# Fewer page transfers, and the gated attention's rows of z loaded during the latent attention

## The chip, the cores and the metric

One core of a Trainium2 chip runs the whole kernel. The metric is the device time of one execution in microseconds, as the median of several runs; lower is better. Everything is float32.

## What is computed

One layer of a hybrid decoder for 512 prompt tokens and 64 sample tokens (8 sequences of 8). The reference, cut to what the change concerns:

```
z = rmsnorm(x) @ w_in                    # columns: latent attention | q, k, v, gate rows of the gated attention
mla_o = latent attention(z[:, :832])     # sample: over 16 pages of 128 cached tokens for each sequence
    s = (q_lat . lat_pool[page_table] + q_rope . kr_pool[page_table]) * ir_pool[page_table] * scale
gla_o = gated linear attention(z[:, 832:], state)
h = x + concat(rmsnorm(mla_o), gla_o) @ w_out
h = h + peer(rmsnorm(h))                 # per token and head: top 16 of 16384 experts; dots with rows of peer_u,
                                         # then the weighted sum of rows of peer_v
y = h + sigmoid(rmsnorm(h) @ w_ple_gate) * (p @ w_ple_proj)
```

The paged cache has, for each token, 256 latents, 64 rotated key values and 8 inverse key norms (inverse RMS).

## The kernel before

The 576 tokens are five tiles: 0 to 3 of the prompt, 4 (`PT`, 64 rows) of the sample. They pass the *front* (input projection, latent attention, gated attention, output projection, query projection, routing) in three groups: [0], [1, 2], [3, 4]. Group 1's input projection (`ahead`, L1208 on TensorE) is woven into group 0's front.

Behind the front runs the expert layer, the bulk of the bytes. For each unit (tile and head; tile 4 packs two heads) GpSimd issues 16 gathers of 128 rows of `peer_u` and 16 of `peer_v` (`gathers`, L2420), 1 MiB each, into a ring of eight buffers: 576 units' dots on VectorE (L1871) and 576 steps of the weighted sum (L1896), 1152 *rows* of work in all. A gather may start once VectorE has used the buffer eight before. A tile's gathers need its routes (`route_ready`), and its rows of `xrow` (L2380, one load for a tile of the prompt).

VectorE and ScalarE do both, the front's steps and the expert rows. VectorE's order is a table: `ROWS_BEFORE` says before which row each step of the front is done; `STEPS_BEFORE` does so for ScalarE, `CHAIN_BEFORE_PIECE` and `CHAIN_BEFORE_COPY` for the weaving in group 0, and `PAGES_BEFORE` says before which gather GpSimd issues each page transfer. Nothing is chosen at run time: an engine waits at the head of its own list.

**Pages (tile 4).** Each sequence's 16 pages come in two halves of eight (`pages_until`, L2402), each by three indirect transfers, of the latents (1 MB), the rope keys (256 KB) and the inverse RMS (32 KB), on GpSimd's queue among the gathers. Five half buffers are in turn. TensorE waits for all three of a half before `turn` (L1000, L1001, transposes), then come `score` (L1012 to L1014), the weighted sum (L1040) and its denominator (L1043). The indices `page_rows` are made by VectorE at the start from `page_table`. The mask `smask` is loaded with the constants (L539).

**Gated attention.** The SyncE queue (SP) waits until all outputs of the group's latent attention are stored and, in groups 0 and 1, its keys are parked in DRAM. Then it issues the gate weights, the state `S0` and the first tile's z (128 x 3088, 1.5 MB) to the one place `gz`. The next tile's z goes out after the first one's `gla_read` and the store of its output `go`; for tile 4 behind the output of the final prompt state too:

```
for t in tiles:
    if t != tiles[0]:
        e.wait_ge(s("gla_read"), t)
    e.dma_start(gz[:ROWS[t], :], z_dram[rows(t), MLA_COLS:IN_COLS]).then_inc(s("gla_z_loaded"), 16)
...
    e.wait_ge(s("gla_o_ready"), t + 1)
```

On VectorE the steps of a tile are: fills (L1464, L1465, first tile alone), gate (L1573, L1574, L1578), levels (L1604 to L1617, L1648, L1654), state update (L1664), output (L1691, L1694). TensorE begins a tile with transposes of z (L1086 to L1090), ScalarE ends it with L2195, which is followed by `gla_read`.

## Time and profile before

| | us |
|---|---|
| median of three runs | 4427.2 |
| lowest and highest | 4423.9, 4427.7 |
| the profiled execution, own time | 4432.5 |
| its span, first to last instruction | 4430.7 |

Mean granted clock of TensorE over the span: 0.719. 1599.5 MB move, 1268.3 of them on GpSimd's queue. The rows below give stretches of this span, in us from its start. A row of a chain or a timeline begins with the start and the duration. In a window's row a busy time in us is followed by the number of instructions begun in it.

### The profile page before, as it was taken

The page shows a single profiled execution, that of the slowest core. Times are in us where ns is not written, and L with a number is a line of the kernel's source. Part 1 is how long each engine was busy: PE and PEld are TensorE (multiplying, and loading weights), DVE is VectorE, ACT ScalarE, POOL GpSimd, SP SyncE. Part 2 cuts the span into 40 slices and gives each one's busy share as a digit, 9 for nine tenths or more (in the row PEclk, how much of TensorE's full clock was granted, in tenths as well). Part 3 has the DMA queues.
Part 4 walks back from the last instruction along what each step waited for, and adds up shares of the span by engine and source line. Part 5 has one row for each costly group of instructions (what it writes and reads, how often), then busy time and mean ns, then how long its engine had stood idle before and what let it go on. Part 6 is the DMA issues. An engine that isn't in the chain of part 4 may idle for free.

```text
span 4430.7 us, 24002 instructions
## 1 busy us (share of the span) xinstructions
PE 2274.9 (51%) x8206; PEld 1357.4 (31%) x8206; DVE 3288.9 (74%) x3698; ACT 516.6 (12%) x1093; POOL 2182.4 (49%) x1232
## 2 busy tenths in 40 slices
PE   8999715424989482678882339720000570000916
PEld 4457403222475131366662213620000230000402
DVE  0130699898566988866889875699999879988682
ACT  2120102122012001211111110100000100001000
POOL 0000365644231546566775563435668547877370
PEclk9999856556999796767665559865555785555957
DMA  8667889988996999979898999998899999999995
GB/s 285 245 234 273 322 351 351 381 360 322 420 388 269 410 414 411 360 284 361 317 379 355 370 367 421 419 366 332 353 399 405 404 422 423 422 403 421 422 418 184
DMA packets 261537, 1599.50 MB, mean 361 GB/s; under 512 B 28019, under 2 KB 49715, under 8 KB 92134
## 3 DMA queue, kind: packets, MB, share of 16 engines
q0 software_dynamic: 176448, 1268.30, 70.8%
q1 hardware_dynamic: 83078, 320.63, 19.2%
q10 hardware_dynamic: 1888, 9.03, 0.5%
q8 instruction: 65, 1.06, 0.1%
q14 instruction: 58, 0.48, 0.0%
HBM read 1554.75 MB, written 42.56 MB: 361 GB/s over the span
## 4 chain that ended last, share of the span: by engine, by line
PE 33%; DVE 27%; DMA 15%; POOL 14%; issue 7%; ACT 2%; SPq 1%; another core or an unknown queue 0%; DVEq 0%; ACTq 0%; POOLq 0%
PE bank L796 15%; POOL ring L2420 13%; DVE total L1896 9%; DVE ring L1871 8%; DMA ring<-in_peer_v,idx_all 5%; PE bank L1208 4%; PE bank L1171 4%; DMA ring<-in_peer_u,idx_all 4%; DMA front<-z_dram 1%; PE bank L770 1%; PE bank L850 1%; POOL front L2402 1%; PE bank L1040 1%; DMA front<-in_cache_k_inv_rms,page_rows 1%; PE bank L1014 1%
## 5 line engine op out<-in xcount | busy, mean ns | idle before, releaser
L1896 DVE SCALAR_TENSOR_TENSOR total<-ring,gate_all,total 128x2048 f32<-128x2048 f32 x571 | 1342.0, 2350 | 190.9 <-DMA ring<-in_peer_v,idx_all 166.4
L2420 POOL DMA_INDIRECT ring<-in_peer_u,idx_all x576 | 1062.8, 1845 | 822.6 <-DVE dots L1871 352.8
L1871 DVE CUSTOM_DVE_ANT_0 ring<-ring,xrow 128x2048 f32<-128x2048 f32 x576 | 1298.2, 2286 | 205.3 <-DMA ring<-in_peer_u,idx_all 202.5
L2420 POOL DMA_INDIRECT ring<-in_peer_v,idx_all x576 | 1003.0, 1741 | 746.4 <-DVE total L1896 327.6
L796 PE MATMUL bank<-front 128*128 128x512 f32 (+3 forms) x2048 | 896.1, 595 | 77.2 <-ACT front L2009 71.8
L770 PE MATMUL bank<-inv_diag,front 128*128 128x128 f32 (+1 forms) x336 | 66.3, 382 | 1286.7 <-DVE inv_diag L1294 1218.7
L796 PEld LDWEIGHTS bank<-front 128*128 128x128 f32 (+1 forms) x2048 | 356.6, 178 | 605.7 <-issue 600.6
L770 PEld LDWEIGHTS bank<-inv_diag,front 128*128 128x128 f32 (+1 forms) x336 | 63.0, 290 | 1292.3 <-DVE inv_diag L1294 1214.2
L1171 PE MATMUL bank<-front 128*128 128x128 f32 (+2 forms) x1536 | 256.7, 329 | 19.1 <-DMA front<-in_peer_w_q 17.4
L1171 PEld LDWEIGHTS bank<-front 128*128 128x128 f32 x1536 | 239.5, 192 | 37.8 <-DMA front<-in_peer_w_q 20.3
L2443 POOL DMA_DIRECT2D ring<-in_w_in x12 | 10.8, 902 | 366.4 <-PE bank L1208 239.2
L1292 DVE RECIPROCAL st<-st 128x1 f32<-128x1 f32 (+1 forms) x20 | 3.2, 161 | 219.2 <-ACT st L1961 219.2
L1208 PE MATMUL bank<-ring 128*128 128x490 f32 x384 | 163.8, 574 | 2.1 <-ACT front L2009 2.1
L2364 ACT ACTIVATE dots<-dots 128x16 f32<-128x16 f32 x36 | 7.7, 215 | 997.9 <-DVE dots L1871 954.1
L834 PE MATMUL bank<-ident,front 128*128 128x128 f32 (+1 forms) x20 | 4.6, 380 | 184.8 <-DVE front L1342 93.1
L1000 PE MATMUL bank<-ident,front 128*128 128x128 f32 x256 | 75.5, 397 | 40.6 <-DMA front<-in_cache_k_inv_rms,page_rows 34.8
L1208 PEld LDWEIGHTS bank<-ring 128*128 128x128 f32 x384 | 70.4, 190 | 74.9 <-issue 71.8
L2380 POOL DMA_DIRECT2D xrow<-xn_dram x6 | 3.4, 576 | 179.1 <-DMA z_dram<-total 102.5
L1116 PE MATMUL bank<-front 128*128 128x128 f32 (+1 forms) x288 | 42.7, 321 | 90.8 <-DVE front L1605 79.6
L1487 DVE MAX8 front<-front 128x8 f32<-128x128 f32 (+1 forms) x80 | 19.2, 280 | 91.7 <-ACT front L2219 91.1
L1331 DVE TENSOR_TENSOR g_mla<-g_mla 128x128 f32<-128x128 f32 x1 | 0.3, 291 | 100.5 <-DMA g_mla<-in_qk_gain_q 100.5
L1040 PE MATMUL bank<-front 128*64 128x256 f32 x256 | 69.7, 440 | 7.9 <-ACT front L2251 7.9
(306 smaller groups left out, 2889.4 us busy)
## 6 DMA issues: line engine op xcount, KB each, us to landing
front<-in_w_in SPq DMA_DIRECT2D x64, 980.0 KB, 6.9
front<-in_w_out SPq DMA_DIRECT2D x48, 1024.0 KB, 9.1
front<-in_peer_w_q SPq DMA_DIRECT2D x48, 1024.0 KB, 13.5
front<-in_w_ple_gate SPq DMA_DIRECT2D x48, 1024.0 KB, 9.0
ring<-in_w_in POOLq DMA_DIRECT2D x12, 1960.0 KB, 10.1
front<-in_w_uq SPq DMA_DIRECT2D x6, 1536.0 KB
ring<-in_peer_u,idx_all POOLq DMA_INDIRECT x576
ring<-in_peer_v,idx_all POOLq DMA_INDIRECT x576
```

Source lines behind the costliest of these rows:

```text
L770: mm = e.matmul(out, row, inv_diag[:R, :R], start=True, stop=True)
L796: mm = e.matmul(bank[4 * sl + c][:R, 0:ncol], XT[:, k, sl * P:sl * P + R], W[:, n % SLABS, c * ncol:(c + 1) * ncol], start=(k == 0), stop= ...
L850: mm = e.matmul(bank[j][:R, 0:2 * QK], cqT[:, slot(t), k, 0:R], wq[:, k, j * 2 * QK:(j + 1) * 2 * QK], start=(k == 0), stop=(k == 3))
L1000: e.transpose(bank[k][:, j * P:(j + 1) * P], latb[:, i, k * P:(k + 1) * P], ident[:, :])
L1014: mm = e.matmul(S, lt[0:ROPE, 2, j * P:(j + 1) * P], qrT[0:ROPE, b, :], start=False, stop=True)
L1040: e.matmul(bank[7][0:NS, 0:KVR], pTs[:, pg, :], latb[:, pg % HALF, :], start=(pg == 0), stop=False)
L1171: mm = e.matmul(bank[j][:, 0:ntok], W[:, n % SLABS, at:at + P], XT[:, k, 0:ntok], start=(k == 0), stop=(k == KD - 1))
L1208: mm = e.matmul(bank[6 + sl][:, 0:IN_BANK], xt[:, k, sl * P:(sl + 1) * P], chunk(n)[:, k % 8, :], start=(k == 0), stop=(k == KD - 1))
L1871: e.tensor_tensor_reduce(out=ring[:, b, :], in0=ring[:, b, :], in1=xrow[:, t % 2, :], scale=1.0, scalar=0.0, op0=ALU.mult, op1=ALU.add, ac ...
L1896: e.scalar_tensor_tensor(out=total, in0=ring[:, b, :], scalar=c1, in1=total, op0=ALU.mult, op1=ALU.add).then_inc(s("summed"), 1)
L2402: e.indirect_dma_start(out=dst.rearrange("p i d -> p (i d)"), out_offset=None, in_=a[pool][0].rearrange("n (r i) d -> (n r) (i d)", r=16), ...
L2420: e.indirect_dma_start(out=ring[:, k % RING, :], out_offset=None, in_=a[("peer_u", "peer_v")[side]][0], in_offset=bass.IndirectOffsetOnAxi ...
```

## The change

1. **Page transfers.** The inverse RMS of all pages goes to a buffer of its own, by eight transfers (one for each sequence, 64 KB) at the program's start on GpSimd's queue. The rope keys come by one transfer of 512 KB for each sequence, with its first half, into one of three buffers. The latents stay as they were, 16 of 1 MB. Index rows are made for sequences (8) and halves (16).
2. **Mask.** `smask` is loaded before `w_uk` of the sample attention, no longer with the constants.
3. **z of the gated attention.** In groups 0 and 1 SP issues the gate weights, `S0` and the first tile's z before it waits for the last output of the latent attention, when the last values are projected (`v_ready`); in group 2 where it did before. The second tile's z goes out once the first one's has landed, to another place: tiles 0, 1 and 4 use `gz_first`, 2 and 3 `gz_other`. The places of the other gated buffers are shuffled for that. TensorE gets a wait for the state of the tile before; VectorE waits for the stores and the parked keys itself before its fills.
4. **Tables.** All five are planned anew.

```
 PAGE_BUFS = 5
+KR_BUFS = 3
...
-PAGES_BEFORE = [390, 396, 396, 399, 399, 415, 419, 431, 431, 442, 447, 453, 463, 469, 469, 480]
+PAGES_BEFORE = [395, 395, 395, 402, 404, 414, 414, 426, 428, 440, 440, 451, 452, 462, 467, 476]
...
-        page_ids = sb("page_ids", [P, 2 * DEC_B * HALF], I32)
-        page_rows = sb("page_rows", [P, 2 * DEC_B], U32)
+        page_ids = ring[:, 4, 0:DEC_B * N_PAGES].bitcast(I32)
+
+        page_rows = sb("page_rows", [P, 3 * DEC_B], U32)
+        page_irms = sb("page_irms", [P, DEC_B, N_PAGES * H_MLA])
...
-            pages_sb.append((carve(HALF, KVR), carve(HALF, ROPE), carve(HALF, H_MLA)))
+            pages_sb.append(carve(HALF, KVR))
+        smask = carve(DEC_B, NS)
+        kr_sb = [carve(N_PAGES, ROPE) for _ in range(KR_BUFS)]
...
-        gz = carve(GLA_COLS, at=0)
+
+        gz_first = carve(GLA_COLS, at=half0)
...
+        gz_other = carve(GLA_COLS, at=0)
+
+        def gz_at(t):
+
+            return gz_other if t == PT - 1 or slot(t) and t != PT else gz_first
...
+        def pages_landed(u):
+
+            return 16 * sum(2 - v % 2 for v in range(u % PAGE_BUFS, u + 1, PAGE_BUFS))
...
-            e.dma_start(smask[:, :, :].rearrange("p a b -> p (a b)"), c["smask"]).then_inc(s("consts_loaded"), 16)
...
+                def gated_loads():
+                    e.dma_start(w_ga[0:GATE_R, :], a["w_gla_a"][0]).then_inc(s("gla_w_loaded"), 16)
+                    e.dma_start(w_ga[GATE_R:GATE_R + 1, :], a["b_gla_a"][0].rearrange("(o n) -> o n", o=1)).then_inc(s("gla_w_loaded"), 16)
+                    if g:
+                        e.dma_start(S0, s_dram).then_inc(s("gla_w_loaded"), 16)
+                    t = tiles[0]
+                    e.dma_start(gz_at(t)[:ROWS[t], :], z_dram[rows(t), MLA_COLS:IN_COLS]).then_inc(s("gla_z_loaded"), 16)
+
...
+                        if hh and t == tiles[-1] and PT not in tiles:
+                            e.wait_ge(s("v_ready"), PHALVES[hh, t] + 1)
+                            gated_loads()
...
                     e.wait_ge(s("sample_qT_psum"), 2)
+                    e.dma_start(smask.rearrange("p a b -> p (a b)"), c["smask"]).then_inc(s("sample_w_loaded"), 16)
                     e.dma_start(wuk_f, a["w_uk"][0].rearrange("(k p) h d -> p k (h d)", p=P)).then_inc(s("sample_w_loaded"), 16)
...
-                e.dma_start(w_ga[0:GATE_R, :], a["w_gla_a"][0]).then_inc(s("gla_w_loaded"), 16)
-                e.dma_start(w_ga[GATE_R:GATE_R + 1, :], a["b_gla_a"][0].rearrange("(o n) -> o n", o=1)).then_inc(s("gla_w_loaded"), 16)
-                if g:
-                    e.dma_start(S0, s_dram).then_inc(s("gla_w_loaded"), 16)
+                if PT in tiles:
+                    gated_loads()
...
-                    if t != tiles[0]:
+                    if t == tiles[0] and len(tiles) > 1:
+                        e.wait_ge(s("gla_z_loaded"), 16 * (t + 1))
+                        e.dma_start(gz_at(t + 1)[:ROWS[t + 1], :], z_dram[rows(t + 1), MLA_COLS:IN_COLS]).then_inc(s("gla_z_loaded"), 16)
+                    if t == PT:
                         e.wait_ge(s("gla_read"), t)
-                    e.dma_start(gz[:ROWS[t], :], z_dram[rows(t), MLA_COLS:IN_COLS]).then_inc(s("gla_z_loaded"), 16)
-                    if t == PT:
...
-                    latb, krb, _ = pages_sb[u % PAGE_BUFS]
+                    latb, krb = pages_sb[u % PAGE_BUFS], kr_sb[u // 2 % KR_BUFS]
                     if n % 2 == 0:
-                        e.wait_ge(s(f"pages_landed{u % PAGE_BUFS}"), 16 * 3 * (u // PAGE_BUFS + 1))
+                        e.wait_ge(s(f"pages_landed{u % PAGE_BUFS}"), pages_landed(u))
...
                     if t:
                         e.wait_ge(s("gla_read"), t)
+                        e.wait_ge(s("gla_state"), H_GLA * t)
...
                 e.wait_ge(s("o_stored"), O_STORED[g])
+                e.wait_ge(s("mla_outputs"), 16 * 2 * (tiles[-1] + 1))
+                e.wait_ge(s("lat_stored"), 16 * (tiles[-1] + 1))
+                if g < LAST:
+                    e.wait_ge(s("keys_parked"), 16 * 6 * (g + 1))
                 e.wait_ge(s("gla_w_loaded"), 32 * (g + 1) + 16 * g)
...
-                    ir = pages_sb[(2 * b + half) % PAGE_BUFS][2].rearrange("p g h -> p (g h)")
+                    if b == 0 and half == 0:
+                        e.wait_ge(s("page_irms_loaded"), 16 * DEC_B)
+                    ir = page_irms[:, b, half * HALF * H_MLA:(half + 1) * HALF * H_MLA]
...
-            link(e.tensor_scalar(page_at, page_at, 16.0, in_page[:, :], ALU.mult, ALU.add))
+            link(e.tensor_copy(page_f, page_ids.rearrange("p (u q) -> p u q", q=N_PAGES)))
+            link(e.tensor_tensor(page_f, page_f, which_page.unsqueeze(1).to_broadcast([P, DEC_B, N_PAGES]), ALU.mult))
+            link(e.tensor_reduce(page_at[:, 0:DEC_B], page_f, AX, ALU.add))
+            link(e.tensor_scalar(page_at[:, 0:DEC_B], page_at[:, 0:DEC_B], float(HALF), in_page[:, :], ALU.mult, ALU.add))
+            halves_at = page_at[:, DEC_B:3 * DEC_B].rearrange("p (u h) -> p u h", h=2)
+            mark(e.tensor_scalar(halves_at[:, :, 0], page_at[:, 0:DEC_B], 2.0, None, ALU.mult))
+            link(e.tensor_scalar(halves_at[:, :, 1], page_at[:, 0:DEC_B], 2.0, 1.0, ALU.mult, ALU.add))
...
+            def pages(dst, pool, tokens, at):
+
+                return e.indirect_dma_start(out=dst, out_offset=None,
+                                            in_=a[pool][0].rearrange("n (r i) d -> (n r) (i d)", i=tokens),
+                                            in_offset=bass.IndirectOffsetOnAxis(ap=page_rows[:, at:at + 1], axis=0))
...
-                    for dst, pool in zip(pages_sb[u % PAGE_BUFS], ("cache_kv_latent", "cache_k_rope", "cache_k_inv_rms")):
-                        e.indirect_dma_start(out=dst.rearrange("p i d -> p (i d)"), out_offset=None,
-                                             in_=a[pool][0].rearrange("n (r i) d -> (n r) (i d)", r=16),
-                                             in_offset=bass.IndirectOffsetOnAxis(ap=page_rows[:, u:u + 1], axis=0))\
+                    b = u // 2
+                    if u % 2 == 0:
+                        if b >= KR_BUFS:
+                            e.wait_ge(s("latT_psum"), 4 * (b - KR_BUFS) + 4)
+                        pages(kr_sb[b % KR_BUFS].rearrange("p i d -> p (i d)"), "cache_k_rope", 2 * HALF, b)\
                             .then_inc(s(f"pages_landed{u % PAGE_BUFS}"), 16)
+                    pages(pages_sb[u % PAGE_BUFS].rearrange("p i d -> p (i d)"), "cache_kv_latent", HALF, DEC_B + u)\
+                        .then_inc(s(f"pages_landed{u % PAGE_BUFS}"), 16)
 
...
             e.wait_ge(s("page_rows_ready"), 1)
+            for b in range(DEC_B):
+                pages(page_irms[:, b, :], "cache_k_inv_rms", 2 * HALF, b).then_inc(s("page_irms_loaded"), 16)
```

How instructions move, at three places. SP in group 1, from the last output stores of the latent attention to the output projection's input; before:

```order
L598 DMA mix_dram<-front 128x512 x2
L606 DMA kt_dram<-front 512x1x256
L607 DMA ktr_dram<-front 256x1x256
L608 DMA v_dram<-front 128x1024
L612 DMA out_ir_p<-ms 128x8 x2
L633 DMA front<-in_w_gla_a 16x512
L634 DMA front<-in_b_gla_a 1x512
L636 DMA front<-s_dram 128x1024
L644 DMA front<-z_dram 128x3088
L655 DMA mix_dram<-front 128x1024
L644 DMA front<-z_dram 128x3088
L655 DMA mix_dram<-front 128x1024
```

and in the change:

```order
L625 DMA mix_dram<-front 128x512
L608 DMA front<-in_w_gla_a 16x512
L609 DMA front<-in_b_gla_a 1x512
L611 DMA front<-s_dram 128x1024
L613 DMA front<-z_dram 128x3088
L625 DMA mix_dram<-front 128x512
L633 DMA kt_dram<-front 512x1x256
L634 DMA ktr_dram<-front 256x1x256
L635 DMA v_dram<-front 128x1024
L639 DMA out_ir_p<-ms 128x8 x2
L670 DMA front<-z_dram 128x3088
L682 DMA mix_dram<-front 128x1024 x2
```

The first z went ahead of the last output of the latent attention, the second ahead of the first gated output.

VectorE in group 1, from the output of the first tile (L1694, now L1728) to the gate of the second (L1573, now L1607); a dot product with a row of peer_u is two rows of this list. Before, where nine dot products stand between the two:

```order
L1691 RECIPROCAL ms<-ms 128x4
L1694 SCALAR_TENSOR_TENSOR front<-bank,ms,front 128x256 x4
L1871 ISA ring,dots<-ring,xrow 128x2048
L1871 ISA dots 128x1
...
L1573 TENSOR_SCALAR front<-bank 128x512
L1574 SCALAR_TENSOR_TENSOR front<-front 128x512
```

and in the change:

```order
L1725 RECIPROCAL ms<-ms 128x4
L1728 SCALAR_TENSOR_TENSOR front<-bank,ms,front 128x256 x4
L1933 SCALAR_TENSOR_TENSOR total<-ring,gate_all,total 128x2048
L1908 ISA ring,dots<-ring,xrow 128x2048
L1908 ISA dots 128x1
L1607 TENSOR_SCALAR front<-bank 128x512
L1608 SCALAR_TENSOR_TENSOR front<-front 128x512
```

Nine rows became two. Counted in rows of expert work done before a step: the fills of group 1 124, now 125; the gate of its second tile 153, now 145; its mix norms 173, now 165. In group 2 the output of tile 3 stands at 528, now 533, the gate of tile 4 at 536, now 543; the last routing step of tile 4 at 848, now 831, the first norm of the embedding at 858, now 840.

GpSimd, where the page transfers begin among the gathers of one unit; before:

```order
L2420 DMA ring<-in_peer_v,idx_all 128x2048 x6
L2402 DMA front<-in_cache_kv_latent,page_rows 128x2048
L2402 DMA front<-in_cache_k_rope,page_rows 128x512
L2402 DMA front<-in_cache_k_inv_rms,page_rows 128x64
L2420 DMA ring<-in_peer_v,idx_all 128x2048 x6
L2402 DMA front<-in_cache_kv_latent,page_rows 128x2048
```

and in the change:

```order
L2465 DMA ring<-in_peer_v,idx_all 128x2048 x11
L2422 DMA front<-in_cache_k_rope,page_rows 128x1024
L2422 DMA front<-in_cache_kv_latent,page_rows 128x2048 x2
L2422 DMA front<-in_cache_k_rope,page_rows 128x1024
L2422 DMA front<-in_cache_kv_latent,page_rows 128x2048
L2465 DMA ring<-in_peer_v,idx_all 128x2048 x5
```

Of three transfers a half, two or one are left, and they begin five gathers later.

## Rows read from the trace of the kernel before

**Rows 1.** The page: busy shares of the engines, and the span in 40 slices.
```profile
PE 2274.9 (51%) x8206; PEld 1357.4 (31%) x8206; DVE 3288.9 (74%) x3698; ACT 516.6 (12%) x1093; POOL 2182.4 (49%) x1232
...
GB/s 285 245 234 273 322 351 351 381 360 322 420 388 269 410 414 411 360 284 361 317 379 355 370 367 421 419 366 332 353 399 405 404 422 423 422 403 421 422 418 184
```

**Rows 2.** Windows: seven stretches, busy us of each engine (instructions), clock, DMA.
```profile
590.00:1385.00 795.00, 439.86 (x1594) 296.46 (x1594) 622.14 (x655) 153.88 (x319) 357.46 (x210) 0.72 0.89 358
...
1883.00:2337.00 454.00, 360.45 (x1873) 292.54 (x1873) 336.18 (x280) 73.35 (x138) 326.70 (x172) 0.67 0.85 336
...
2900.00:3410.00 510.00, 9.84 (x79) 9.18 (x77) 496.16 (x711) 12.10 (x27) 311.29 (x178) 0.51 0.92 367
3410.00:4330.00 920.00, 273.25 (x712) 132.39 (x712) 766.91 (x528) 45.99 (x112) 592.66 (x315) 0.65 1.01 417
```

**Rows 3.** Waits of POOL: us in total, times, longest us.
```profile
POOL ring L2443 <- PE bank L796: 127.3, 1, 127.3
POOL xrow L2380 <- DMA z_dram<-total: 102.5, 1, 102.5
POOL xrow L2380 <- DVEq L1789: 76.5, 1, 76.5
```

**Rows 4.** Chain that ended last, between the tiles of group 1: start us, us, what.
```profile
962.91 0.31 ACT ms L2195
...
965.51 12.85 DMA front<-z_dram
...
978.40 0.38 PE bank L1086
```

**Rows 5.** The page, costliest groups: the two kinds of row work.
```profile
L1896 DVE SCALAR_TENSOR_TENSOR total<-ring,gate_all,total 128x2048 f32<-128x2048 f32 x571 | 1342.0, 2350 | 190.9 <-DMA ring<-in_peer_v,idx_all 166.4
...
L1871 DVE CUSTOM_DVE_ANT_0 ring<-ring,xrow 128x2048 f32<-128x2048 f32 x576 | 1298.2, 2286 | 205.3 <-DMA ring<-in_peer_u,idx_all 202.5
```

**Rows 6.** Windows: two stretches of group 1's projections.
```profile
1100.00:1150.00 50.00, 50.00 (x118) 22.16 (x117) 27.74 (x24) 0.00 (x0) 11.25 (x12) 1.00 1.01 421
...
1300.00:1385.00 85.00, 74.80 (x368) 64.83 (x366) 41.68 (x90) 22.25 (x57) 2.54 (x4) 0.90 0.61 233
```

**Rows 7.** Timeline of DVE, fills and last state update of group 1's first gated attention.
```profile
887.57 0.17 DVE L1464 MEMSET front<- 17x128 f32 x1
...
959.84 0.86 DVE L1664 SCALAR_TENSOR_TENSOR front<-front,bank 128x256 f32<-128x256 f32 x2
```

**Rows 8.** Waits of PE, 2337 to 2560 us.
```profile
PE bank L1086 <- DMA front<-z_dram: 27.0, 1, 27.0
```

**Rows 9.** Groups by line, 1883 to 2337 us: POOL's transfers of rope keys and inverse RMS.
```profile
L2402 POOL DMA_INDIRECT front<-in_cache_k_rope,page_rows x16 | 38.8, 2422 | 4.9 <-issue 4.9
L2402 POOL DMA_INDIRECT front<-in_cache_k_inv_rms,page_rows x16 | 34.9, 2180 | 4.9 <-issue 4.9
```

**Rows 10.** Waits of PE and then of POOL, 1883 to 2337 us.
```profile
PE bank L1000 <- DMA front<-in_cache_k_inv_rms,page_rows: 34.8, 6, 12.1
...
POOL ring L2420 <- DVE total L1896: 57.9, 10, 21.8
```

**Rows 11.** The same chain, 1880 to 2460 us: the four landings of page transfers.
```profile
2003.31 10.95 DMA front<-in_cache_k_inv_rms,page_rows
...
2063.80 3.50 DMA front<-in_cache_k_inv_rms,page_rows
...
2148.10 9.70 DMA front<-in_cache_k_inv_rms,page_rows
...
2207.11 8.30 DMA front<-in_cache_k_inv_rms,page_rows
```

**Rows 12.** Timeline of POOL, issues of three page transfers.
```profile
2000.81 0.94 POOL L2402 DMA_INDIRECT front<-in_cache_kv_latent,page_rows  x1 [0.30 <-issue]
...
2003.31 9.13 POOL L2402 DMA_INDIRECT front<-in_cache_k_inv_rms,page_rows  x1 [0.30 <-issue]
...
2066.19 2.08 POOL L2402 DMA_INDIRECT front<-in_cache_kv_latent,page_rows  x1 [0.30 <-issue]
```

52 lines of the change are left out of this document (25 added, 27 removed), and 64 rows, old and new, of tables (CHAIN_BEFORE_PIECE, ROWS_BEFORE).

## The prediction

> **What bounds the kernel now.** I began with the page's busy shares and forty slices [rows 1]. No engine is full over the span: VectorE (DVE) has 74%, TensorE (PE) 51%, GpSimd (POOL) 49%. But the DMA engines move 422 GB/s in the best slices and hold that in the last quarter. The windows by stretch say why [rows 2]. From 3410 us on the gathers run at 417 GB/s: DMA bounds. From 2900 to 3410 us DVE is busy 496.2 of 510 us: routing the last tiles beside the row work bounds. In the latent attention of the sample tile (1883 to 2337 us) neither is full: DVE 336.2 of 454 us, DMA 336 GB/s. In 590 to 1385 us, group 1's front, DMA moves 358 GB/s. Idle DMA time at 422 GB/s: 454 x (1 - 336/422) = 92.5 us in the first of these, 795 x (1 - 358/422) = 120.6 us in the second. Time can be won only where both DVE and DMA stand partly idle.
>
> One thing more bounds group 1's front. POOL stood 76.5 us before one load of xrow [rows 3]: it had fetched all that tile 0 and its routes allowed, and waited for the first route of tile 1. So what shortens the chain from group 1's latent attention to its route comes off the total one to one, until that wait is gone. Before the first gather PE is the bound, with work waiting.
>
> **The change part by part.**
>
> *z of the second tile of group 1: -15.0 us.* Before, SP issues that load only after the output store of the first tile. ACT's root that raises gla_read ended at 963.2 (962.91 + 0.31), z landed at 978.36, PE began at 978.40 [rows 4]. In the change the load goes out while tile 1 runs, to a place of its own, and PE starts at about 963.4: 978.4 - 963.4 = 15.0 us. PE's new wait for gla_state is over by then: DVE's last L1664 ended at 960.7 [rows 7]. Queued behind it on PE is only this tile's own work. Nothing is lost on DVE: between the two tiles it took nine rows, now two; the seven, at 2.29 to 2.35 us each [rows 5], are done later, in the stretch where PE projects (1056 to 1385 us). There DVE is idle anyway and DMA, over 1300 to 1385 us, moves 233 GB/s [rows 6], 38 us of idle transfer time; seven rows ask 7 x 2.49 = 17.4 us of it (1 MiB at 422 GB/s).
>
> *First tile's z, gate weights and state, fetched earlier: 0.* PE could start sooner, but DVE does its fills at 887.57 [rows 7], when the table lets it, and the table still does so at the same row (124 before, 125 now). DVE's added waits for the small outputs and parked keys cost nothing: SP waited for the same ones before it issued the loads for which DVE then waited.
>
> *z of tile 4 (group 2): 0, bounds -27.0 and 0.* PE waited 27.0 us for it [rows 8], behind the state's output. The load now goes out during tile 3. But no route is waited for later: POOL's xrow waits are two, this tile's is not among them [rows 3]. The new table also puts ten rows, not eight, between the two tiles' steps on DVE. A shorter chain with slack behind it gives nothing, so I take the upper end.
>
> *Pages: -12.5 us, bounds 0 and -34.8.* Before, 48 page transfers stand in POOL's queue among the gathers of that stretch. The change leaves 24: the 16 of inverse RMS become 8 at the program's start, the 16 of rope keys become 8. By their means that takes 34.9 + 38.8/2 = 54.3 us off POOL, and 24 gaps of 0.30 make 61.5 [rows 9, 12]. PE waited 34.8 us in six waits for pages [rows 10]. Four landings stand on the chain that ended last, 10.95, 3.50, 9.70 and 8.30 us [rows 11], each behind the third transfer of its half. Per half 1.5 transfers fewer at 2.08 + 0.30 us (what most cost beside DVE's row work [rows 12]) is 3.57 us; four make 14.3. Back go two larger key transfers (256 KB more, 0.6 us each at 422 GB/s) and 0.6 for the mask, now loaded just ahead of w_uk, for which PE waits: -14.3 + 1.2 + 0.6 = -12.5. The lower end is all that PE waited; the upper that the ring of eight row buffers takes the place of the page: POOL waited 57.9 us for DVE's sums there too [rows 10]. I stand nearer the middle, since only four waits were on the chain.
> The Trainium skill, DMA: Bandwidth & Descriptors, section on the anatomy of a DMA from the GpSimd queue, gives a fixed part of about 2.0 us and bytes over 436 GB/s. By this a 32 KB transfer lands 2.1 us after it starts, and four of them off the chain would be 8.4 us, a total of some 4406. The trace's four landings are longer (3.50 to 10.95 us), so the row decides.
>
> *The eight early transfers: 0.* POOL's first wait is 127.3 us long, for PE [rows 3]; they fit ahead of it. They move 0.5 MB, 1.2 us of DMA, beside a stretch where PE is the chain. *Mask out of the constants: 0.* One load of 256 KB less ahead of x, 0.6 us of DMA at 422 GB/s.
>
> *Replanned tables: 0, upper end +45.* The routing of tile 4 and the first embedding's norms are packed: by row 840, not 858. Those 18 rows lie in or just after the stretch where DVE is full [rows 2]. DVE's work is the same, only sooner, and DMA still has idle time to give.
>
> **Sum**, against the profiled execution's own time: 4432.5 - 15.0 - 12.5 = 4405.0. The median of the three runs is 5.3 us below that execution, so I forecast 4400 (4399.7).
>
> **Rivals.**
> *More: POOL was the limit of the latent stretch.* For it: the same kind of issue takes 0.94, 2.08 or 9.13 us [rows 12], the long one while DVE ran row after row without a gap, and DMA stands idle meanwhile. Removing an issue removes such a stall. Then all 34.8 us of page waits go, 22 more than forecast: 4378; with some of tile 4's z, 4370. Against: POOL also waited 57.9 us for DVE there.
> The Trainium skill, SBUF: State Buffer, section Who interferes with whom, says that a DVE instruction with two SBUF inputs blocks a GpSimd instruction only if that one reads SBUF, and then fully. An indirect transfer reads its indices there. The 9.13 us issue agrees with a full block, and by this rule this rival is what should happen.
> *Less: the pages give nothing.* The next gather's buffer, still held by DVE, is what POOL then waits for. 4427.2 - 15.0 = 4412.
> *None: the weights pay.* In 1100 to 1150 us DMA is at 421 GB/s, gathers and w_out together [rows 6]. Seven more gathers there are 17.4 us of transfer; if they delay the weights, not the idle end, PE's projection gets longer by as much, and group 1's 15 us are gone. With the pages giving nothing too: 4427. Against: PE's projection shows no such wait, it is busy 50 of 50 us there [rows 6]. It is also the case in which the change does not do what it says: a z load held in SP's queue behind the keys' stores and landing late, which at 15 us to spare would also end here.
> *Slower: the packed routing.* In 2900 to 3410 us DVE is at 97%, DMA at 367 GB/s. If routing steps are set closer than the ring of eight rows can bridge, DMA stops, and no later stretch gives that back, for there DMA is full. At worst each of 18 rows costs its 2.49 us: 4400 + 45 = 4445. It decides from 12 rows on (30 us against the 27.5 won). Against: ring and DVE rate stay, and the table was already dense.
>
> **How the numbers follow.** Forecast (4388 to 4411): 0.40. More (4365 to 4388): 0.19. Less (4412): 0.14. None (4427): 0.15. Slower (around 4445): 0.12. 0.2% is 8.9 us, about what a measurement of this kernel can tell from no change. The first three are faster: 0.73; same 0.15; slower 0.12. The range leaves out the far end of "more" and nearly all of "slower": 4368 to 4430.
>
> **What would show it.** In the profile after: PE's wait for z between the tiles of group 1 gone, the next gate matmul about 15 us after the last output matmul less than before; POOL's wait for the second xrow earlier by 15 us and about 60 long; 24 page issues, not 48, in the latent stretch, a page wait of PE of some 20 us or less, that stretch shorter than 454 us; DVE's full stretch not longer than before by more than 10 us. I am wrong if POOL's route wait ends where it did, if PE waits in L796 for weights, or if the latent stretch keeps its length with POOL waiting longer for DVE.

## The result and the profile after

The changed kernel takes 4347.0 us (median of four runs, 4345.2 to 4349.3) against 4426.4 us for the kernel before (four runs, 4423.9 to 4427.7): the ratio is 0.9822, interval 0.9805 to 0.9839, some 79 us faster. I forecast 4400 and a range down to 4368: the sign is right, the size is not, and the time lies below that range. The profiled execution has a span of 4346.4 us (before 4430.7) and a mean granted clock of 0.727 (before 0.719).

The page of the changed kernel, busy shares and forty slices (compare [rows 1]):

```profile
PE 2255.6 (52%) x8206; PEld 1342.1 (31%) x8206; DVE 3289.2 (76%) x3700; ACT 521.2 (12%) x1097; POOL 2204.8 (51%) x1216
...
GB/s 295 251 221 286 307 357 362 415 326 338 424 424 294 423 424 411 348 353 362 407 377 357 347 402 413 409 346 343 399 362 404 424 423 422 422 402 423 423 415 181
```

DVE has the same work (3289 us), PE about 19 us less of busy time for the same 8206 matmuls. The slices that were at 284 and 317 GB/s in the latent stretch are gone.

Windows of the changed kernel, the stretches of [rows 2] between the same steps of VectorE; the columns are the same:

```profile
578.00:1350.00 772.00, 437.83 (x1589) 295.17 (x1590) 628.42 (x648) 148.90 (x310) 372.60 (x213) 0.73 0.92 373
1847.00:2253.00 406.00, 333.82 (x1865) 271.49 (x1865) 328.01 (x275) 70.92 (x135) 307.56 (x149) 0.73 0.93 374
2820.00:3330.00 510.00, 14.32 (x105) 13.42 (x103) 501.32 (x725) 14.87 (x30) 296.88 (x174) 0.52 0.92 370
3330.00:4250.00 920.00, 276.13 (x712) 133.85 (x712) 764.86 (x516) 51.02 (x116) 600.89 (x318) 0.65 1.01 416
```

Group 1's front is 23 us shorter, the latent stretch 48 us. The two last stretches are as before. Not all of that reaches the end: the rows of work are the same 1152, and what one stretch does sooner the next may not need sooner. So I also counted the rows of work (in the changed kernel L1908, L1933 and, for the first step of a sum, L1931) in each trace, from 0, and compared when row n ended. This table gives the end time in the kernel before, and the difference to it, in us:

| row of work | before | changed |
|---|---|---|
| 96 | 815.3 | -20.8 |
| 192 | 1148.5 | -4.9 |
| 256 | 1468.0 | -38.0 |
| 384 | 1894.0 | -36.9 |
| 480 | 2265.3 | -80.5 |
| 640 | 2823.0 | -77.6 |
| 832 | 3402.0 | -67.2 |
| 928 | 3702.9 | -83.6 |
| 1151 | 4339.3 | -84.4 |

In these two traces about 37 us come from group 1's front and 41 to 44 us from the latent stretch; my terms were 15.0 and 12.5. Some 22 us of the second gain are there only against this trace of the kernel before, not against its second one (below).

The signs I had named. Waits of POOL in the changed kernel (compare [rows 3]), and one line of its timeline:

```profile
POOL xrow L2417 <- DMA z_dram<-total: 102.5, 1, 102.5
...
POOL xrow L2417 <- DVEq L1823: 60.4, 1, 60.4
```

```profile
1350.97 0.56 POOL L2417 DMA_DIRECT2D xrow<-xn_dram  x1 [60.38 <-DVEq L1823]
```

The wait for tile 1's route is 60.4 us long, as forecast (some 60), but that is luck: it ends 33 us earlier than the 1384.0 of before, not 15, and it also begins 17 us earlier. Its length does not come from the early z. With both edits under the old tables it is as long as before, and with all z late under the new tables as short as here (the kernels "changed, tables as before" and "changed, all z late" below):

```profile
POOL xrow L2417 <- DVEq L1823: 77.8, 1, 77.8
```

```profile
POOL xrow L2416 <- DVEq L1822: 62.1, 1, 62.1
```

In every kernel with the new rows of group 1 it is 57 to 62 us long, in every one with the old rows 77 to 78.

The page transfers and PE's wait for them, 1847 to 2253 us (compare [rows 9, 10]):

```profile
L2422 POOL DMA_INDIRECT front<-in_cache_kv_latent,page_rows x16 | 27.8, 1740 | 11.8 <-PE bank L1071 8.1 <-issue 3.7
L2422 POOL DMA_INDIRECT front<-in_cache_k_rope,page_rows x8 | 15.2, 1902 | 2.4 <-issue 2.4
```

```profile
PE bank L999 <- DMA front<-in_w_uk: 16.0, 1, 16.0
...
PE bank L1027 <- DMA front<-in_cache_kv_latent,page_rows: 9.1, 3, 5.9
```

24 issues, and 9.1 us of page waits instead of 34.8.

### The profile page after: what moved, and what is told of

Same layout as the page of the kernel before. It is cut to its first block, busy times and chain, and to the rows that moved or that the text cites. A ratio compares the mean times of both kernels' runs of the same rounds, so it can differ in the third digit from the quotient of the medians.

```text
span 4346.4 us, 23992 instructions
## 1 busy us (share of the span) xinstructions
PE 2255.6 (52%) x8206; PEld 1342.1 (31%) x8206; DVE 3289.2 (76%) x3700; ACT 521.2 (12%) x1097; POOL 2204.8 (51%) x1216
## 4 chain that ended last, share of the span: by engine, by line
PE 34%; DVE 30%; POOL 16%; DMA 10%; issue 7%; ACT 2%; SPq 0%; DVEq 0%; ACTq 0%; POOLq 0%
PE bank L823 18%; POOL ring L2465 15%; DVE ring L1908 11%; DVE total L1933 9%; PE bank L1199 4%; DMA ring<-in_peer_u,idx_all 3%; PE bank L1236 3%; DMA ring<-in_peer_v,idx_all 3%; PE bank L797 1%; PE bank L877 1%; DMA front<-in_cache_kv_latent,page_rows 1%; PE bank L1027 1%; PE bank L947 1%; PE bank L1041 1%; DVE front L1531 1%
## 5 line engine op out<-in xcount | busy, mean ns | idle before, releaser
L1933 DVE SCALAR_TENSOR_TENSOR total<-ring,gate_all,total 128x2048 f32<-128x2048 f32 x571 | 1342.0, 2350 | 179.5 <-DMA ring<-in_peer_v,idx_all 154.6
L2465 POOL DMA_INDIRECT ring<-in_peer_v,idx_all x576 | 1074.1, 1865 | 699.0 <-DVE total L1933 358.2
L1908 DVE CUSTOM_DVE_ANT_0 ring<-ring,xrow 128x2048 f32<-128x2048 f32 x576 | 1297.5, 2287 | 172.9 <-DMA ring<-in_peer_u,idx_all 171.0
```

Source lines behind the costliest of these rows:

```text
L1908: e.tensor_tensor_reduce(out=ring[:, b, :], in0=ring[:, b, :], in1=xrow[:, t % 2, :], scale=1.0, scalar=0.0, op0=ALU.mult, op1=ALU.add, ac ...
L1933: e.scalar_tensor_tensor(out=total, in0=ring[:, b, :], scalar=c1, in1=total, op0=ALU.mult, op1=ALU.add).then_inc(s("summed"), 1)
L2465: e.indirect_dma_start(out=ring[:, k % RING, :], out_offset=None, in_=a[("peer_u", "peer_v")[side]][0], in_offset=bass.IndirectOffsetOnAxi ...
```

## Experiments

Two theories stood at the start. **Edits:** early z and fewer page transfers win the time, the tables only follow. **Pair:** VectorE works through a fixed list, so an edit that makes an input early pays only as far as the table also puts the step that uses it at an earlier row; and an earlier row pays only if the input is there. All eighteen runs, with the kernel before run beside them on the same chip (rows with the same time of the kernel before make one block, run on one chip; the changed kernel itself was run in the first comparison and in "changed, again"):

| kernel | median us | kernel before | ratio, interval |
|---|---|---|---|
| changed, tables as before | 4385.7 | 4415.1 | 0.9925 to 0.9965 |
| before, new tables | 4391.1 | 4415.1 | 0.9941 to 0.9967 |
| changed, 48 page transfers | 4363.0 | 4415.1 | 0.9873 to 0.9909 |
| changed, all z late | 4367.4 | 4415.1 | 0.9882 to 0.9916 |
| **changed, again** | 4345.1 | 4411.0 | 0.9826 to 0.9864 |
| before, again (one run) | 4406.9 | 4411.0 | |
| new tables for group 1 alone | 4364.0 | 4411.0 | 0.9859 to 0.9903 |
| tail of the table as before | 4345.2 | 4411.0 | 0.9814 to 0.9864 |
| first z late | 4351.1 | 4407.4 | 0.9848 to 0.9894 |
| z of tile 2 late | 4366.8 | 4407.4 | 0.9878 to 0.9926 |
| old start of group 1 | 4359.8 | 4407.4 | 0.9860 to 0.9904 |
| gaps between dot products | 4347.1 | 4407.4 | 0.9841 to 0.9883 |
| z of tile 4 late | 4353.1 | 4424.8 | 0.9829 to 0.9859 |
| new start, old rows of group 1 | 4373.5 | 4424.8 | 0.9871 to 0.9901 |
| page table as before | 4400.1 | 4424.8 | 0.9925 to 0.9955 |
| early z alone, tables as before | 4401.7 | 4424.8 | 0.9948 to 0.9975 |
| new page table, old rows | 4352.6 | 4412.6 | 0.9834 to 0.9874 |
| pages two gathers sooner | 4351.4 | 4412.6 | 0.9840 to 0.9877 |

### The two kernels again

> The changed kernel once more, unedited, so that the parts are compared on one chip: 0.982 of the kernel before, as in the first comparison.

> The kernel before once more, unedited, for its trace on this chip. By every theory the times of its rows of work lie within some 10 us of the first trace's; where they do not, that much of the differences so far is the chip and not the edit.

The changed kernel repeats within 2 us, and its rows of work end within 3 us of the first trace's. The kernel before does not, and I had expected its traces within some 10 us: its second trace (span 4405.1) is within 3 us of the first up to row 384, 23.6 us ahead at row 480 and 25.0 at the end. Its medians on the chips used lie between 4407.4 and 4426.4. So some 22 of the 84 us between the first two traces are how the old kernel's latent stretch happened to go in that one. Where I compare traces below, it is with the second one of before: there the changed kernel (second trace) is 35.3 us ahead at row 384, 52.6 at row 640 and 62.1 at the end.

### Edits alone, tables alone

The edit of the first: the five lists of the kernel before in the changed kernel; of the second: the new lists in the kernel before.

```
 # changed kernel
-ROWS_BEFORE, STEPS_BEFORE, PAGES_BEFORE, CHAIN_BEFORE_PIECE, CHAIN_BEFORE_COPY = new
+ROWS_BEFORE, STEPS_BEFORE, PAGES_BEFORE, CHAIN_BEFORE_PIECE, CHAIN_BEFORE_COPY = as before
```

> The changed kernel with all five tables of the kernel before. Theory A (the edits themselves win the time, the tables only follow): 4345 to 4360 us, nearly all of the 79 us. Theory B (the edits make room, and only the new tables use it: they start group 1's front earlier and set the latent stretch closer): 4395 to 4412 us, that is 15 to 30 us won. Theory C (the tables alone): 4427 us.

> The kernel before with all five tables of the changed one: the replanning alone. Theory A: 4420 to 4440 us, no gain. Theory B: part of the gain, 4385 to 4410 us (group 1's earlier start of some 24 us survives, but VectorE then waits in its closer list for z and for pages). Theory C: 4347 us, all of it.

4385.7 and 4391.1 us: 29.4 and 24.0 us below the kernel before by medians (by the ratios 24 and 20). Together they give 66 us on the second chip (4411.0 to 4345.1) and 79 on the first. What the pair theory expected came true for the second kernel; the first came out 9 us below its lower end, on a chip where the kernel before is 11 us faster too. That edits alone, or tables alone, carry the gain falls: each has under half of it. But the two halves nearly make the whole. By the last row of the traces the edits alone are 28.0 us ahead of the second trace of before, the tables alone 22.9, both together 62.1. So 11 us of the 62 are there only when both are (13 of 66 by medians). The pair theory holds for that part; the larger part each half wins by itself.

### Early z, taken apart

All late: the loads moved back to their places in the kernel before. First late: `gated_loads()` moved back. Tile 2 or tile 4 late: the second tile's load again behind the first one's output.

```
-                    if t == tiles[0] and len(tiles) > 1:
+                    if t == tiles[0] and len(tiles) > 1 and not (t + 1 == 2):
                         ... load of z of t + 1
+                    if t != tiles[0] and t == 2:
+                        e.wait_ge(s("gla_read"), t)
+                        ... load of z of t
```

> The changed kernel with z, gate weights and state loaded where they were before, in all groups (the first tile's behind the last output of the latent attention, the second's behind the first one's output), pages and tables as changed. By my forecast 15 us for tile 2 and nothing else: 4362 us. If the closer tables of group 1 need the early z, more: group 1's gated chain was 33 us earlier in the changed kernel, so up to 4380 us. If tile 4's z counts too (27 us of wait before), up to 4400 us.

> The changed kernel with only the first tile's gate weights, state and z in groups 0 and 1 back behind the last output of the latent attention; the second tile's follows it and still goes out early. By my prediction this part is worth 0: 4346 us. Rival: the new table puts VectorE's gated steps at earlier rows, so that a late first z makes VectorE itself stand still at the gate of tile 1; then part of the 21 us that all late loads cost (4367 us against 4346): 4352 to 4360 us.

> The changed kernel with only tile 2's z (second of group 1) behind the first tile's read and the store of its output, as before; tile 4's stays early. By my prediction this is worth 15 us: 4361 us. By the traces so far, with all z late VectorE stood 19.3 us at the gate of tile 2, a step that the new table puts 8 rows earlier: 4361 to 4366 us, and rows 160 to 256 some 18 us later.

> The changed kernel with only tile 4's z back behind the output of tile 3 and the final prompt state. By my prediction (no route is waited for later, a shorter chain with slack gives nothing) 0: 4346 us. Rival, the end that I left out of the sum: TensorE's 27.0 us of wait come off tile 4's chain, which the new table sets closer, so up to 4372 us with the late load.

All late costs some 21 us (4367.4 against 4345.1 to 4347.0), the first z alone 4 to 6, tile 2's z alone 20 to 22. (The changed kernel was not run in these blocks, so this rests on its two medians elsewhere.) Of tile 2's, 12.0 us are there at row 384 and 20.8 at row 640; what adds the rest on the way was not looked for. Tile 4's costs 6 to 8 by medians, but nothing by the ratio (0.9844 against 0.9845 for the changed kernel on its own chip), and its trace ends 5.6 us behind: between 0 and 8, not settled. PE waited 38.5 us for that z in its trace, and little of it came through.

What a late z does under the new table is in the waits of DVE of the kernel with all z late, 860 to 1000 us (columns: us in total, times, longest):

```profile
DVE front L1606 <- ACT front L2203: 19.1, 1, 19.1
```

L1606 is the gate of tile 2. The new table sends VectorE there at row 145, before at 153; z is not in, and VectorE itself stands 19.1 us with all its rows behind that step. What an early z does under the old table is in the waits of PE of the changed kernel with old tables, same stretch:

```profile
PE bank L1123 <- ACT front L2194: 45.3, 2, 44.7
PE bank L1128 <- DVE front L1608: 32.0, 2, 21.2
```

The wait for z has become one of 21.2 us for the same gate step, which VectorE's list reaches only at row 153. The timeline of DVE gives the start of that step in three kernels (the changed one, all z late, old tables):

```profile
954.04 0.69 DVE L1607 TENSOR_SCALAR front<-bank 128x512 f32<-128x512 f32 x1 [0.27 <-ACT front L2204]
```

```profile
971.97 0.69 DVE L1606 TENSOR_SCALAR front<-bank 128x512 f32<-128x512 f32 x1 [19.07 <-ACT front L2203]
```

```profile
979.73 0.69 DVE L1607 TENSOR_SCALAR front<-bank 128x512 f32<-128x512 f32 x1
```

From the fills of the group (874.3, 875.7, 883.1 us) that is 79.8, 96.3 and 96.6 us; in the kernel before 99.5 (887.6 to 987.0, [rows 7] has the fill). Counted from the fills, each half of the change wins 3 us at this step, both together 20. Counted from the start of the span the step begins at 987.0 us before (984.2 in the second trace), 979.7 with the old tables, 972.0 with all z late and 954.0 in the changed kernel, since the fills move too. With the old tables POOL's route wait ends at 1373.8 us (before 1384.0 and 1381.7), 8 to 10 us earlier.

### The table of group 1, taken apart

```
+ROWS_BEFORE = before[:96] + new[96:]                 # old start
+ROWS_BEFORE = new[:96] + before[96:347] + new[347:]  # new start, old rows
```

In the first of the two, ScalarE's first six numbers are as before too. In the second, three entries at the seam are one or two higher, so that the list does not fall.

> The changed kernel with the table of before for VectorE's first 96 steps (as far as row 95 of work: group 0's last routes and the start of group 1's latent attention) and ScalarE's first six numbers; all later steps as in the new table. The new table lets group 1's front start at row 18, the old one at row 25. If that earlier start carries group 1's gain beyond the early z (the changed kernel was 17.5 us ahead at row 96): 4358 to 4364 us. If the later rows of the table carry it (tile 2's gate at row 145, not 153): 4346 to 4350 us.

> The mirror of the old-start kernel: VectorE's first 96 steps as in the new table, its steps 96 to 346 (rows 95 to 345, the gated attention, output and query projection of group 1) as before, all later steps, ScalarE's and the pages' tables as new. If the two parts of the table add up (the early start some 12 us by row 384, the closer rows the other 12): 4357 to 4362 us. If the start alone carries it: 4347 us. If it is lost without the closer rows: 4366 us or more.

Without the earlier start (row 25 instead of 18) 4359.8 us, 13 to 15 worse. Without the closer rows 4373.5 us, 27 to 28 worse than the changed kernel's medians in other blocks, 20 worse than the kernel with tile 4's z late in its own; there PE waits again for VectorE at the gate, 860 to 1000 us:

```profile
PE bank L1096 <- DVE front L1576: 32.2, 2, 21.4
```

The traces at row 384, in us ahead of the second trace of before, separate the three things that make up group 1's gain:

| early z | closer rows | early start | ahead at row 384 |
|---|---|---|---|
| yes | no | no | 11.5 |
| yes | no | yes | 11.9 |
| yes | yes | no | 23.6 |
| yes | yes | yes | 35.3 |
| no | yes | yes | 17.0 |

The start is worth nothing (0.4 us) while VectorE's later rows are the old ones, and 11.7 us with the closer ones. The closer rows are worth 12.1 us with the old start and 23.4 with the new. Early z is worth 18.3 us under the new table. If the two parts of the table added up, the kernel without the closer rows would have been at 4357 to 4362 us. They don't: an explanation that fits is that a chain that starts sooner ends sooner only if none of its steps is held at an old row. One pair of traces does not fit so well: the kernel before with the new tables, which has no early z either, is only 10.5 us ahead at row 384, not 17.0. Where these 6.5 us come from was not tested.

### Pages and the tables of the latent stretch

48 transfers: keys and inverse RMS in halves again, three transfers for each half page set.

```
-                    if u % 2 == 0: pages(kr_sb[...], "cache_k_rope", 2 * HALF, b)
-                    pages(pages_sb[...], "cache_kv_latent", HALF, DEC_B + u)
+                    for dst, pool in (latents, half of the keys, half of the inverse RMS):
+                        pages(dst, pool, HALF, DEC_B + u)
```

> The changed kernel with 48 page transfers in the latent stretch again (rope keys and inverse RMS in halves, each half by three transfers), all else as changed. If pages were worth my 12.5 us: 4359 us. If GpSimd was the limit of that stretch, as my rival had it (34.8 us and more; the trace shows the stretch about 35 us shorter, with denser tables): 4380 to 4395 us. If pages gave nothing: 4347 us.

4363.0 us: the pages are worth 16 to 18 us by medians and 13 by the traces at the last row. My 12.5 was sized about right for the new tables.

The early z alone, with 48 transfers and the old tables:

> The changed kernel with the five tables of before and 48 page transfers in the latent stretch: early z alone, the first two terms of my prediction without any replanning. My forecast is -15.0 us for it; the trace with old tables and both edits was 11.5 us ahead at row 384: 11 to 15 us faster than the kernel before on the same chip, that is 4395 to 4402 us against 4411, and the rest up to the 4385.7 of both edits (10 to 16 us) is what the page edit gives under the old tables, where I forecast 12.5.

4401.7 us, 23.1 below the kernel before by medians, 17 by the ratio (0.9961), where I had expected 11 to 15; its trace is 11.1 us ahead at row 384 and 12.4 at the end. Against the kernel with both edits under the old tables (24 by its ratio, 29.4 by medians) the page edit has 6 or 7 us, by the traces' last rows 15.5. These numbers are too near the spread to be split further; the two edits together under the old tables are 24 to 29 us, and my sum was 27.5.

The tables there: those of before behind group 1 (VectorE's steps from 347 on, ScalarE's from unit 27 on, pages), then the same but with the new page table, then the old page table alone, then new pages two gathers sooner:

```
+ROWS_BEFORE = new[:347] + before[347:]; STEPS_BEFORE = new[:27] + before[27:]
+PAGES_BEFORE = before          # first and third kernel, new in the second
+PAGES_BEFORE = [n - 2 for n in new]   # fourth; rows new in the third and fourth
```

> The changed kernel with the new tables only as far as group 1's routing (347 of VectorE's 705 steps), the tables of before behind it. If each stretch's gain is its own: group 1's part stays (38 us by row 256, 37 at row 384 in the changed kernel) and the latent stretch keeps only what the page edit gives under the old table; with my 12.5 us for that, 4427 - 37 - 12.5 = 4377 us. If the latent stretch needs no new table: 4347 us.

> The changed kernel with the row and step tables of before behind group 1, as in the kernel of 4364.0 us, but with the new page table. If the page table carries the latent stretch's 19 us by itself: 4346 us. If it is the pair that counts (pages that keep ahead of VectorE's rows): the new page table is in the mean earlier than the old one, so TensorE's page waits (18.1 us there) fall, and the time stays between: 4352 to 4364 us. With the pair as cause and the old rows as the limit it does not get worse than 4364 us.

> The changed kernel with only the table of page transfers as before (before which gather each of the 16 goes out); the row and step tables stay new. The old tables behind group 1 cost 18.9 us (4364.0 against 4345.1). If the page table is what carries that: 4360 to 4365 us. If VectorE's rows carry it: 4345 to 4350 us.

> The changed kernel with each page transfer two gathers sooner. The old page table, up to 11 gathers later, cost 54 us. If pages still bind the stretch, this wins a little: 4338 to 4344 us. If TensorE's remaining 8.1 us of page waits are covered, or the queue then waits for a page buffer instead of gathering: 4346 to 4356 us.

4364.0, 4352.6, 4400.1 and 4351.4 us. The old rows and the old page table behind group 1 together cost 17 to 19 us (I had expected 0 or 30); the new page table gives 11 of them back, 8 by the traces. The old page table under the new rows costs 53 to 55 against the changed kernel's medians elsewhere, 47 against the kernel with tile 4's z late in its own block: thirteen of the sixteen halves come up to 11 gathers later (three come 3 to 5 sooner) while most of VectorE's steps sit 2 to 7 rows earlier. I had expected 15 to 20 at most. So the old page table is worse under new rows than under old ones (4400.1 against 4364.0): this is the clearest sign of a pair. The chip is one on which the kernel before, too, is slow (4424.8), and part of the cost may come from that. Waits of PE in that kernel, and its window from the start of the stretch to the fills of the gated attention:

```profile
PE bank L1027 <- DMA front<-in_cache_kv_latent,page_rows: 51.1, 6, 13.5
```

```profile
1844.00:2303.00 459.00, 355.66 (x1865) 289.22 (x1865) 328.02 (x273) 71.14 (x135) 287.61 (x149) 0.67 0.83 329
```

The same window in the changed kernel and in the second trace of the kernel before:

```profile
1847.00:2252.00 405.00, 333.82 (x1865) 271.49 (x1865) 327.29 (x272) 70.92 (x135) 307.09 (x149) 0.73 0.93 373
```

```profile
1885.00:2318.00 433.00, 354.84 (x1865) 288.17 (x1865) 336.98 (x280) 73.57 (x138) 328.28 (x170) 0.69 0.90 354
```

The first number after the stretch is its length, the next PE's busy time. All have 1865 matmuls, but PE is busy 334, 355 or 356 us for them. The granted clock goes with it: 0.73, 0.69, 0.67. In all rows of the next table busy time times clock lies between 237 and 245 us (worked out from them), so the busy time differs by the clock and not by the work. PE is busy for most of this stretch; that its slower matmuls lengthen it as its waits do is my reading, and no run tested it. Over the kernels:

| kernel | stretch, us | PE's page waits | PE busy | clock |
|---|---|---|---|---|
| before, first trace | 457 | 34.8 | 359.4 | 0.66 |
| before, second trace | 433 | 25.1 | 354.8 | 0.69 |
| page table as before | 459 | 51.1 | 355.7 | 0.67 |
| edits, old tables | 423 | 27.2 | 343.8 | 0.71 |
| before, new tables | 414 | 14.6 | 341.6 | 0.71 |
| changed, 48 transfers | 415 | 16.9 | 339.6 | 0.71 |
| changed | 405 | 9.1 | 333.8 | 0.73 |
| pages two gathers sooner | 401 | 6.6 | 332.4 | 0.73 |
| early z alone, tables as before | 439 | 27.0 | 348.2 | 0.69 |
| gaps between dot products | 401 | 2.1 | 339.1 | 0.72 |
| new tables for group 1 alone | 437 | 18.1 | 364.8 | 0.67 |
| new page table, old rows | 429 | 3.0 | 352.2 | 0.69 |

From the first to the changed kernel the stretch loses 52 us: 25.7 of page waits and 25.6 of PE's busy time. From the second trace of before it loses 28: 16.0 of page waits and 21.0 of busy time, and PE's other idle time grows by 9. So the even split of the first pair is no rule. In the rows above the last two, fewer page waits mostly go with a higher clock; the kernel with gaps, with the fewest of those waits and 0.72, does not quite fit. The last two show that pages are not the only thing that it goes with: there VectorE's steps come at the old rows, and PE's clock is 0.67 to 0.69 even with 3.0 us of page waits. What goes with the clock is a correlation here; no run held all else fixed. Two gathers sooner gains nothing more (4351.4; the stretch is 4 us shorter and the end is not earlier).

### The packed routing

```
+ROWS_BEFORE = new[:552] + before[552:]
```

> The changed kernel with the table of before from VectorE's step 552 on (rows 584 and later: the last routing and the first embedding's norms no longer packed). My rival (packed steps stop the gathers, 2.49 us for each of 18 rows) would make this faster than the changed kernel, by up to 45 us: 4302 us. If the packing costs nothing in the end (row 832 was 18 us late in the changed kernel's trace and row 928 on time again): 4347 us. If the packing was a gain: above 4352 us.

4345.2 against 4345.1 us: no difference. The traces show what happens in between. At row 832 the changed kernel is 43.8 us ahead of the second trace of before and this one 56.5, at row 928 60.2 and 58.4. The packed steps delay the rows by some 18 us between rows 800 and 832, and 16 of them come back by row 928, when the old table does its steps. Windows of this kernel, the stretch in which VectorE is full:

```profile
2820.00:3330.00 510.00, 8.60 (x71) 7.94 (x70) 496.21 (x709) 14.67 (x29) 311.09 (x179) 0.51 0.92 366
```

VectorE is busy 496 of 510 us there, 501 in the changed kernel: it is full with either order.

### Are GpSimd's long issues a bound?

In the latent stretch single issues of GpSimd last up to 11.6 us. POOL and DVE of the changed kernel (second trace), timeline from 2165 us:

```profile
2167.68 11.60 POOL L2465 DMA_INDIRECT ring<-in_peer_v,idx_all  x1 [3.00 <-DVE dots L1908]
2179.58 3.11 POOL L2465 DMA_INDIRECT ring<-in_peer_v,idx_all  x1 [0.30 <-issue]
```

```profile
2167.33 2.28 DVE L1908 CUSTOM_DVE_ANT_0 ring<-ring,xrow 128x2048 f32<-128x2048 f32 x1
...
2176.18 2.28 DVE L1908 CUSTOM_DVE_ANT_0 ring<-ring,xrow 128x2048 f32<-128x2048 f32 x1
...
2178.39 1.28 DVE L1572 TENSOR_TENSOR front<-front,bank 128x1088 f32<-128x1088 f32 x1
```

Five dot products run end to start (2167.33 to 2178.4), and the issue ends only when VectorE has gone on to an instruction with one input in PSUM. The experiment gives VectorE a gap after each dot product of rows 384 to 544:

```
                     e.tensor_tensor_reduce(... dots ...)
+                    if 384 <= rows_taken[0] < 544:
+                        link(e.memset(breath[:, :], 0.0))     # 1 x 1, and a wait for its end
                     row_taken()
```

> The changed kernel with a one-element fill of VectorE, and a wait for its end, behind each dot product of rows 384 to 544 (some 80). In the traces GpSimd's longest issues (4.4 to 14 us, 9 of them in this stretch) all last while VectorE runs dot products with no gap between them, and end with the burst. If the gap is what lets GpSimd in, no issue in these rows is longer than some 3 us. If those stalls bound the stretch, the time falls by 5 us or more, 4336 to 4341 us, although VectorE has some 10 us more to do; if the ring of eight rows covers them: 4346 to 4356 us.

The same place in this kernel, POOL:

```profile
2167.46 2.89 POOL L2468 DMA_INDIRECT ring<-in_peer_v,idx_all  x1 [4.98 <-DVE dots L1909]
2170.66 2.05 POOL L2468 DMA_INDIRECT ring<-in_peer_v,idx_all  x1 [0.30 <-issue]
2173.02 2.05 POOL L2468 DMA_INDIRECT ring<-in_peer_v,idx_all  x1 [0.30 <-issue]
```

One fill of 0.06 us with a wait for its end lets GpSimd in. Of nine issues over 4 us between 1600 and 2400 us (66 us) two are left (14 us), one of them ahead of row 384, where nothing was added; POOL's busy time in the stretch falls from 307 to 271 us. The time stays: 4347.1 us. In the changed kernel the stalls are real and do not bound the time; that it is the ring of eight rows that covers them is inferred. In the kernel before, with twice the page transfers, the gaps were not tried.

## Why the prediction was right or wrong

**z of the second tile of group 1, -15.0:** right in part. The load goes out early and PE's wait for z is gone, but it does not come off POOL's route wait one to one: that wait is as long as before (77.8 us) and begins and ends 8 to 12 us sooner when the tables are the old ones. The gate step stands at row 153 of VectorE's list there, and PE waited 21.2 us for it. All early z together was worth 11 to 13 us at row 384 under the old rows; with the closer rows tile 2's z alone is worth 20 to 22 us. My 15.0 lies between and fits neither.

**First tile's z, 0:** 4 to 6 us. I said the table does the fills at the same row. It does (124 and 125), but the rows themselves now come 13 us earlier, and then a late z costs a little. A row number is not a time.

**z of tile 4, 0, bounds -27 and 0:** 0 to 8 us, within the bounds.

**Pages, -12.5:** 13 to 18 us under the new tables, 6 to 15.5 under the old ones, so the size was about right; the way I built it left something out. I added up transfers on four landings of the chain. With all changes together the stretch got shorter by PE's page waits and also by PE's busy time at a higher clock: 25.7 and 25.6 us of 52 between the first two traces. The clock of that stretch (0.67) stood in [rows 2], and I did not price it.

**Sum of the edits, -27.5:** with the old tables 24 by the ratio, 29.4 by medians. The sum was right for the edits under the old tables, a kernel that was not the one to be forecast.

**"Replanned tables: 0, upper end +45": this is the step that failed.** I looked at the tables for a cost alone and saw it in the packed routing. They bring most of what is missing from 27.5 to 66 (second chip) or 79 us (first chip): by the last row of the traces 22.9 us by themselves, 34.1 on top of the edits. Without the earlier start of group 1 13 to 15 us are gone, without its closer rows 27 to 28, without the new tables behind group 1 17 to 19, each taken away by itself; the parts overlap and do not add up. Part of it stood in the comparison of the orders: tile 2's gate 8 rows earlier, its mix norms 8. The rest stood in the lists themselves: the start of group 1 7 rows earlier, most steps of the latent stretch 2 to 7. I had the rows and asked neither what the earlier steps win by themselves nor which of them an early input made possible.

**Early transfers and mask, 0:** POOL stood 11.9 us for the index rows at the start, well inside its long wait for PE; PE's wait for w_uk is 16.0 us, 14.7 before, where I had charged 0.6.

**Rivals.** *More* came nearest in its result (all but 9.1 of the 34.8 us of page waits went). Its mechanism is not what bounds the changed kernel: taking GpSimd's long issues away there changes nothing. For the kernel before it was not tried. The Trainium skill, SBUF — State Buffer, section Who interferes with whom, says that an instruction of VectorE with two SBUF inputs contends with one of GpSimd that reads SBUF, and that the lock is exclusive. The issue of 11.60 us agrees, though the page speaks of one instruction and the row shows five in a burst. That this should show in the time did not follow. *Less* and *None* fall with the two kernels under old tables and with 48 transfers. *Slower* falls with the tail of before: the delay at row 832 is there (13 us between those two traces; 18 us from row 800 to 832 in the first comparison) and is given back by row 928. I had argued that no later stretch gives it back since DMA is full there; but what was delayed was VectorE, whose old table had the same steps still to do.

One thing stays open: why the kernel before has a latent stretch of 457 us in one trace and 433 in another, with the same order. Both have long page waits (34.8 and 25.1 us); the changed kernel, with 9.1 and 8.1, has 405 us in both of its traces.

## What to carry to other kernels

Where an engine works through a fixed order, never price a replanned table at nothing: list the steps that moved past rows and ask of each what had kept it there. Price inputs that arrive early and steps placed early, each alone and both as a pair; here (by the traces) the two edits were worth 28 us alone, the tables 23, all together 62. When waits of TensorE go from a stretch that it bounds, compare its busy time for the same matmuls too, for the granted clock may move with them. Time a copy of the old kernel on the same chip: here its median moved by 19 us over six blocks of runs, and the new one's by 2 over two.

## What was unexpected of the hardware

An indirect issue of GpSimd takes 0.94 us alone, about 2.05 beside single dot products with a gap behind each, and as long as the whole burst when they run end to start: 11.60 us over five of them. An added fill of 0.06 us with a wait for its end, after each dot product, ends that for all but one of the eight issues over 4 us in the latent stretch. The clock granted to TensorE over the latent stretch ranged from 0.66 to 0.73 for the same 1865 matmuls, and their busy time from 365 to 332 us.
